# Input projection of a hybrid decoder step: groups of four 128-column items, 512 prompt columns per product, sample tokens as the stationary operand

## The reference, cut to what matters

```python
def mixer_inputs(x, norm_w, w_in, a_q_norm, a_k_norm):
    xn = rms_norm(x, norm_w)
    u, o, mz, ig, fg, q, kv, g, az = jnp.split(xn @ w_in, SPLIT_AT, axis=-1)
    q = rms_norm(q.reshape(B, T, A_HEADS, A_DH), a_q_norm)
    ...
    g = jax.nn.sigmoid(g).reshape(B, T, 3, A_HEADS)
```

## Time and profile before

| | us |
|---|---|
| median of 3 runs | 2227.49 (2226.57 to 2228.03) |
| the profiled execution | 2227.76 |
| its span in the trace | 2226.1 |
| PE busy | 2051.2, 92% of the span |
| DVE busy, ACT busy | 830.4 and 697.4 |
| first to last product of line 250 | 12.5 to 718.3 |

### The profile page before, as it was taken

How to read it: one execution, slowest core, us unless ns; L and a number is a source line. 1 busy time by engine, 2 the same in 40 slices (tenths; PEclk the granted TensorE clock), 3 DMA queues, 4 the chain that set the end, 5 groups by cost and what they waited for, 6 DMA issues and landing times. The chain is left out here.

```text
span 2226.1 us, 34268 instructions
## 1 busy us (share of the span) xinstructions
PE 2051.2 (92%) x13409; PEld 1658.3 (74%) x13409; DVE 830.4 (37%) x1639; ACT 697.4 (31%) x1328; POOL 50.7 (2%) x99
## 2 busy tenths in 40 slices
PE   7999999999999799968997799999997699999998
PEld 7999999999999455655554354544444599989997
DVE  6233235423332334526563134433334422242332
ACT  6332223333332222205663223332222321142222
POOL 0000000000000100000000000000000011100000
PEclk9999999999999788858998899999997799999999
DMA  5452233333331433220123768888864642223320
GB/s 190 163 187 79 87 98 98 107 102 107 99 112 53 155 140 140 82 106 29 58 75 128 262 221 277 294 298 301 301 243 152 228 147 77 81 86 107 99 73 22
DMA packets 163699, 315.00 MB, mean 142 GB/s; under 512 B 18893, under 2 KB 68430, under 8 KB 160466
## 3 DMA queue, kind: packets, MB, share of 16 engines
q1 hardware_dynamic: 143656, 278.98, 37.2%
q10 hardware_dynamic: 19882, 33.83, 4.3%
HBM read 280.75 MB, written 40.26 MB: 144 GB/s over the span
## 5 line engine op out<-in xcount | busy, mean ns | idle before, releaser
L250 PE MATMUL mm<-x_hi,w_hi 128*128 128x288 f32 x1696 | 368.3, 299 | 14.2 <-DVE w_lo L381 14.2
L250 PE MATMUL mm<-x_hi,w_lo 128*128 128x288 f32 x1696 | 363.9, 296 | 0.0
L250 PE MATMUL mm<-x_lo,w_hi 128*128 128x288 f32 x1696 | 363.8, 296 | 0.0
L250 PEld LDWEIGHTS mm<-x_hi,w_hi 128*128 128x128 f32 x1696 | 274.4, 189 | 15.8 <-issue 12.5
L250 PEld LDWEIGHTS mm<-x_hi,w_lo 128*128 128x128 f32 x1696 | 273.9, 189 | 0.0
L250 PEld LDWEIGHTS mm<-x_lo,w_hi 128*128 128x128 f32 x1696 | 273.8, 189 | 0.0
L381 DVE TENSOR_TENSOR w_lo<-w_raw,w_hi 128x1024 fp32r<-128x1024 f32 x106 | 129.8, 1225 | 384.8 <-ACT w_hi L280 384.8
L1515 PE MATMUL s_pH<-wide,cw_sample 128*128 128x512 f32 x512 | 244.5, 619 | 16.2 <-DMA wide<-pages 13.7
L1997 PE MATMUL o_mm<-o_feat_hi,o_w_hi 128*128 128x288 f32 x1024 | 224.7, 301 | 23.6 <-DVE o_feat_lo L2072 19.4
L1997 PE MATMUL o_mm<-o_feat_lo,o_w_hi 128*128 128x288 f32 x1024 | 221.0, 298 | 0.0
L1997 PE MATMUL o_mm<-o_feat_hi,o_w_lo 128*128 128x288 f32 x1024 | 220.7, 297 | 0.0
(11 more groups left out here) (402 smaller groups left out, 2296.3 us busy)
## 6 DMA issues: line engine op xcount, KB each, us to landing
wide<-pages SPq DMA_DIRECT2D x256, 256.0 KB, 3.6
w_raw<-w_in SPq DMA_DIRECT2D x106, 512.0 KB, 3.9
s_kv<-pages SPq DMA_DIRECT2D x128, 256.0 KB, 11.1
s_kv<-pages ACTq DMA_DIRECT2D x128, 256.0 KB, 8.1
o_w_raw<-w_out SPq DMA_DIRECT2D x16, 1024.0 KB, 8.6
o_w_raw<-ple_gate SPq DMA_DIRECT2D x16, 1024.0 KB, 6.7
m_state<-state SPq DMA_DIRECT2D x4, 2056.0 KB, 12.8
state_sample<-m_state SPq DMA_DIRECT2D x4, 2056.0 KB, 6.6
```

The lines of the kernel that those rows point to most:

```text
L250: last = nc.tensor.matmul(mm[:, s % 3, y, 0:HALF], w[:, m % RING, kk, :], f[:, k, y * HALF:(y + 1) * HALF], start=k == 0 and i == 0, stop= ...
```

## The change

The 53 items are put into 13 groups of four and one group with the gate item alone; val moves from behind the gate to the end. A unit is now 2 k-blocks of a group's 512 columns (the gate: 8 k-blocks of 128), still 512 KB, and there are still 106 of them: 8 for a group of four, 2 for the gate. The four items of a group accumulate side by side in four PSUM banks.

For the 512 prompt tokens PE runs one 512-column product where it ran two of 288: for each unit 4 items x 2 k-blocks x 3 = 24. For the 64 sample tokens the roles turn: x_hi and x_lo of the sample tokens are stationary (128 columns, the low part in new columns of `x_hi`), and the weights of the four items stream, 512 columns at once: for each k-block one "wide" product against w_hi and one with the 64 high columns against w_lo, so 4 per unit. They end in one bank (`tail`), token-major. ACT copies it to `sums` (`summed`), and PE turns it back with the stacked identity `stack`, which also adds the halves (`fold`, four float32 matmuls of 64 columns for each group); DVE then scales the result (`sample`). The gate's sample part is computed as before, as 48 products of 64 columns.

`lanes()` writes out which unit (slot) carries which step of which item. The rings are now raw 3, hi 3, lo 2, staging 5. The sum of squares for the norm is taken by PE after unit 2.

```diff
-        mm = ps("mm", [P, 3, 2, CH])
+        mm, tail, turned = ps("mm", [P, 4, CH]), ps("p_tail", [P, CH]), ps("p_turned", [P, 4, TSA])
...
+    for g, group in enumerate(GROUPS):
+        end = max(v for v, (x, _) in enumerate(UNITS) if x == g)
...
+            put(end, "prompt", base + i)
+        if not gate:
+            put(end + 1, "fold", g)
+            for i in range(len(group)):
+                put(end + 2, "sample", base + i)
+        for i in range(len(group)):
+            x = end + 2 * i + (8 if gate else 0)
+            put(x + 2, "first", base + i)
+            put(x + 3, "aside", base + i)
+            put(x + 4, "second", base + i)
+            put(x + 5, "store", base + i)
...
+            def fold(g):
+                pe.wait_ge(sums_ready, nfold(g))
...
+                for i in range(4):
+                    last = nc.tensor.matmul(turned[:, i, :], sums[:, i * P:(i + 1) * P], stack[:], start=True, stop=True)
...
+            def unit(m):
...
+                pe.wait_ge(whi_done, m + 1)
+                pe.wait_ge(wlo_done, m + 1)
+                for i in range(n):
+                    if c == 0 and g:
+                        free = start_of(g - 1) + min(i + 1, len(GROUPS[g - 1]))
+                        pe.wait_ge(prompt_out, free)
...
+                        for y, (w, x) in enumerate(((hi, xhi), (hi, xlo), (lo, xhi))):
+                            last = nc.tensor.matmul(mm[:, i, :], w[:, kk, own], x[:, k, 0:TP], start=k == 0 and y == 0, stop=k == KD - 1 and y == 2)
...
+                if n == 4:
+                    for k, wide in ((ks[0], c == 0), (ks[1], c == 0), (ks[0], c > 0), (ks[1], c > 0)):
+                        if wide:
+                            last = nc.tensor.matmul(tail[:], xhi[:, k, TP:T + TSA], hi[:, k % 2, :], start=k == 0, stop=k == KD - 1)
+                        else:
+                            last = nc.tensor.matmul(tail[0:TSA, :], xhi[:, k, TP:T], lo[:, k % 2, :], start=False, stop=False)
...
+                last.then_inc(unit_done, 1)
+
+            for s in range(LAST + 1):
+                if s < NU:
+                    unit(s)
+                if s == 2:
                     pe.wait_ge(ones_ready, 1)
                     pe.wait_ge(added, KD - 1)
...
             def low(m):
-                if m >= 2 * NI:
+                if m >= NU:
                     return
                 dve.wait_ge(whi_done, m + 1)
-                if m >= RING:
-                    dve.wait_ge(half_done, m - RING + 1)
-                v.tensor_tensor(wlo[:, m % RING], raw[:, m % RING], whi[:, m % RING].bitcast(F32), ALU.subtract).then_inc(wlo_done, 1)
+                if m >= LO:
+                    dve.wait_ge(unit_done, m - LO + 1)
+                v.tensor_tensor(wlo[:, m % LO], raw[:, m % RAW], whi[:, m % HI].bitcast(F32), ALU.subtract).then_inc(wlo_done, 1)
...
+            def prompt(j):
                 kind, n = ITEMS[j]
-                dve.wait_ge(half_done, 2 * j + 2)
...
+                dve.wait_ge(item_done, j + 1)
...
+                v.tensor_tensor(dst, src, rstd[:, 0:TP], ALU.mult).then_inc(prompt_out, 1)
...
             def first(j):
                 kind, n = ITEMS[j]
+                if kind == "u":
+                    convolve(j)
                 if kind in ("u", "z", "az"):
                     dve.wait_ge(sig_ready, nth(("u", "z", "az"), j))
...
+            for s in range(2, LAST + 1):
+                low(s + 2)
+                for what, j in LANES.get(s, []):
+                    if what == "prompt":
+                        prompt(j)
+                    elif what == "sample":
+                        sample(j)
+                    elif what == "first":
+                        first(j)
+                    elif what == "second":
+                        second(j)
```

More of the change, by code:

```diff
@@ L188, in _ @@
                 sp.dma_start(x[:, 4 * i:4 * i + 4, :], a["x_fm"][:, 4 * i:4 * i + 4, :]).then_inc(x_in[i], 16)
[L189 to L199, removed]
+                load(i)
+            for s in range(LAST + 1):
+                load(s + 3) if s else None
+                for what, j in LANES.get(s, []):
+                    if what == "store":
+                        store(j)
+                if s % 2 == 0 and 8 <= s < 8 + 2 * NB:
+                    sp.dma_start(o["win_kept"][s // 2 - 4], a["win_rows"][s // 2 - 4, TS:WIN, :]).then_inc(B.win_kept, 16)
+            for i in range(SLOTS):
+                sp.wait_ge(kv_out[i], 16 * sum(1 for j in range(NI) if ITEMS[j][0] in STORED and j % SLOTS == i))
             sp.wait_ge(row_out, 32 * nth(("o", "z"), NI - 1))
@@ L216, in aside @@
                     pe.wait_ge(sq_ready, nth(NORMED, j))
-                    for h in range(2):
-                        last = nc.tensor.matmul(aux[:, h, 0:HALF], pair[:], sq[:, h * HALF:(h + 1) * HALF], start=True, stop=True)
+                    for part, out in both(sq):
+                        last = nc.tensor.matmul(out, pair[:], part, start=True, stop=True)
                 elif kind == "gate":
@@ L231, in aside @@
                         dst = aux[0:w, t // 4, (t % 4) * P:(t % 4) * P + P]
-                        last = nc.tensor.transpose(dst, stg[:, j % 3, t0:t0 + w], B.ident[:])
+                        last = nc.tensor.transpose(dst, stg[:, j % SLOTS, t0:t0 + w], B.ident[:])
                 last.then_inc(aux_done, 1)
[L235 to L253, removed]
@@ L254, in _ @@
+            for s in range(LAST + 1):
+                if s < NU:
+                    unit(s)
+                if s == 2:
                     pe.wait_ge(ones_ready, 1)
                     pe.wait_ge(added, KD - 1)
-                    for y in range(2):
-                        last = nc.tensor.matmul(aux[:, y, 0:HALF], B.ones[:], rk[:, y * HALF:(y + 1) * HALF], start=True, stop=True)
+                    for part, out in both(rk):
+                        last = nc.tensor.matmul(out, B.ones[:], part, start=True, stop=True)
@@ L323, in second @@
                         act.wait_ge(normal, nth(NORMED, j) - 1)
-                    last = s_.activation(halved(rk[:]), aux[:, :, 0:HALF], ACT.Ln, bias=B.eps[:, 0:1], scale=1.0 / AD)
+                    for part, read in both(rk):
+                        last = s_.activation(part, read, ACT.Ln, bias=B.eps[:, 0:1], scale=1.0 / AD)
                     last.then_inc(aux_read, 1)
@@ L357, in _ @@
                     high(3)
-            high(4)
             act.wait_ge(ssq_done, 1)
-            step(s_.activation(halved(rstd[:]), aux[:, :, 0:HALF], ACT.Ln, bias=B.eps[:, 0:1], scale=1.0 / D))
+            for part, read in both(rstd):
+                last = s_.activation(part, read, ACT.Ln, bias=B.eps[:, 0:1], scale=1.0 / D)
+            step(last)
             s_.activation(rstd[:], rstd[:], ACT.Exp, scale=-0.5).then_inc(rs_ready, 1)
[L362 to L368, removed]
+            for s in range(2, LAST + 1):
+                high(s + 2)
+                for what, j in LANES.get(s, []):
+                    if what == "fold":
+                        summed(j)
+                    elif what == "first":
+                        first(j)
+                    elif what == "second":
+                        second(j)
         @block.vector
@@ L428, in convolve @@
                 empty(j)
+                dve.wait_ge(prompt_out, j + 1)
                 dve.wait_ge(evac, j + 1)
```

188 lines of the change are left out of this document (128 added, 60 removed).

## The result

| | before | after |
|---|---|---|
| median, us | 2227.76 (2226.57 to 2230.68) | 2325.85 (2322.97 to 2325.91) |
| span of the profiled execution | 2226.1 | 2324.1 |
| last product of the projection starts | 718.3 | 811.8 |
| next stage's first instruction | 725.49 | 821.69 |

The ratio is 1.0438, interval 1.0425 to 1.0451: the change makes the kernel 98 us slower, where 49.5 slower was forecast (2277), and the result lies 6 us above the range. Of the 98, 93.5 are there by the last product (after: the second of a pair that starts at 811.60), and the stages behind the projection take 2.6 of the rest.

The account below looks back on a forecast made before the run. The prediction took PE's stream of products as the projection's only bound. Products -33.4, folds +14, group starts +56 (standing plus clock), first 50 us +7.9 and end +5 gave +49.5 on 2227.76: forecast 2277 us, range 2240 to 2320.

Parts of the forecast that it names:

- products, gate included: PE's projection products: 2960 at 0.216 us plus 48 short ones, 645.8 against 679.2 before, so -33.4 us.
- folds: PE's 13 x 4 float32 matmuls turning the sample sums, with switches between kinds: +14 us, between 8 and 20.
- standing at group starts: PE waits at 13 group starts for DVE's eviction, behind `low` and earlier steps: 50.3 us in sum.
- clock behind them: Half clock on PE after the two u-group stops of 8.8 us, 2.9 each: +5.8 us, nothing for the others.
- first 50 us: Projection start: later x and `w_lo`, PE waiting 6.3 us for the additions, then half clock: +7.9 us, between 4 and 9.
- end: Stage's end: val comes last, so DVE's evictions and the transposes follow the last product: +5 us, between 2 and 8.
- the first rival: PE's products: 0.0135 us is a fixed cost of every `fp32r` product, 0.227 each; total 2310 us, chance 0.13.
- The cold row: Profile row from PE's cold start: 288 columns in 0.240 us, columns at 1.2 GHz and no more.
- The rival without standing: Group starts: DVE has evicted before PE needs the bank, so the 56 us go; 2221 us, chance 0.08.

Follow-up runs that it names:

- sums_first: `evict_first` plus unit 4's weights prepared earlier, the norm's sum after unit 3, and ACT's copy of sample sums ahead of the last u sigmoids: 2239.79 us, ratio 1.0058.
- forms: The changed kernel with 24 extra products of varied number form and width ahead of each fold, to price them: fp32r of 512 columns 0.228 us each.
- after_again: The changed kernel executed once more without any edit, to compare the clock behind the same 13 stops: 2323.32 us.
- evict_first: The changed kernel with DVE doing the eviction and the steps it needs ahead of `low` in each group's last slot: 2261.8 us, ratio 1.0173.
- lo3: The changed kernel with three slots of `w_lo` instead of two and two of raw weights instead of three, DVE's order unchanged: 2258.37 us, ratio 1.0151.

## Why the prediction came out where it did

| term | forecast | measured | from |
|---|---|---|---|
| products, gate included | -33.4 | +0.5 | 104 x 6.38 + 48 x 0.2267 + 48 x 0.110 against 679.2 |
| folds | +14 (13) | +9.6 (12) | 7.18 - 6.38 each in `sums_first`; the 13th is in the end |
| standing at group starts | +50.3 | +52.7 | 50.5 idle and 13 x 0.17 of drain |
| clock behind them | +5.8 | +21 | the same stretches in `sums_first` are 73.6 shorter; less 52.7 |
| first 50 us | +7.9 | +7.5 | unit 4 at 50.27, 12.0 beyond 12.8 + 4 x 6.38; less 4.8 before; 0.3 for 12.8 against 12.5 |
| end | +5 | +1.9 | 95.4 at the next stage's first product, less 93.5 |
| other stages | 0 | +2.6 | 98.0 of span less 95.4; the output projection alone +3.9, the others less |
| not assigned | | +2 | |

**Products: the step that failed first, 34 of the 48.5 us missed.** The prediction took 0.216 for an `fp32r` product of 512 columns, and 0.2267 was measured. The two facts it rested on were right: 0.0135 beside the columns in the old products, next to nothing in a pass of a float32 matmul. The error was to carry the float32 pass over to `fp32r` because both read 4 bytes a column, and to explain the 0.0135 away as a load that 288 columns don't cover. `forms` shows it to be a fixed time of `fp32r`, from 256 to 512 columns; that is the first rival, to which the prediction gave a chance of 0.13. That one put the term at -1, and +0.5 was measured. The cold row that spoke for it was the nearer evidence, being of the same number form. The sum shows why nothing is gained. Fewer products carry less of the fixed time (5088 x 0.0135 = 69 before, 2960 x 0.0133 = 39 after: -29). But 53,000 more columns are streamed (+22), the gate's 48 short products pay the floor of 0.110 (+4), and a unit has 0.03 at its switches (+3). The prediction had 8 in place of the 39 (2960 x 0.0027).

**Clock: the second, 15 us.** The forecast put a price only behind the two stops of 8.7 us, and nothing behind the eleven shorter ones, because in one row PE restarted at full pace after 2.90 us of idle time. Eleven of 13 stops lost 1.6 to 2.8 us each, both of 2.08 us among them, and `after_again` shows some of them the other way round. One restart was no bound for a cost that varies. The very stop of that row came out otherwise in the kernel after: the output projection, whose code is the same, stands at this place for 5.31 us and restarts at half clock. First PE of after, then two of its windows, to be set beside the earlier trace rows:

```profile
1889.45 0.82 PE L2103 MATMUL o_mm<-o_feat_hi,o_w_hi 128*128 128x288 f32 x2 [5.31 <-DVE o_w_lo L2172]
```
```profile
1888.00:1892.00 4.00, 2.55 (x11) 2.58 (x12) 2.01 (x2) 1.96 (x2) 1.19 (x1) 0.54 0.03 10
1892.00:1896.00 4.00, 4.00 (x21) 4.00 (x21) 2.29 (x1) 0.53 (x1) 0.24 (x1) 0.61 0.01 2
```

From the first to the last start of that line the stage takes 456.6 us, for 452.7 before. The same stop is 4.6 to 5.6 us long in every kernel made from the change, and a later one, at 2077.84, is 2.08 for 1.30 before. Why the first is 2.90 before was not settled.

**Right: where PE stands, and why.** All 13 stops, for the order and for the two slots; the first of 2.08 (2.2 forecast with 0.17 drain), the two behind u groups of 8.65 and 8.64 (8.8 forecast). `evict_first` and `lo3` take away the same stops from two sides. The DVE view at the longest one reads as the forecast had it, `low`, the convolution, the sigmoids' 2.18, the product, the eviction:

```profile
395.19 1.23 DVE L470 TENSOR_TENSOR w_lo<-w_raw,w_hi 128x1024 fp32r<-128x1024 f32 x1 [3.54 <-PE p_tail L315]
396.33 0.54 DVE L529 TENSOR_SCALAR p_stage<-upad,convw,convb 128x512 f32<-128x512 f32 x1
...
402.23 0.76 DVE L569 TENSOR_TENSOR p_stage<-p_stage,p_square 128x576 f32<-128x576 f32 x1 [2.18 <-ACT p_square L399]
402.90 2.48 DVE L502 TENSOR_TENSOR upad<-mm,p_rstd 128x512 f32<-128x512 f32 x4
```

The rival without standing fell with this, and no wait came up inside the groups. The start (four units by 50.27, 49.7 forecast, a stop of 5.93 for 6.3) came as worked out, but for a slip in the prediction: 49.7 lies 13.0 beyond 12.5 + 4 x 6.05 and not 12.7. Folds and end were sized too high, 7.5 together, which took that much off the miss. What was not foreseen is the wait of `tail` for ACT's copy: hidden in `after` behind the longer stop, it costs 14 us once that is gone.

## What to carry to other kernels

Price a new shape from a row of the same number form (here `fp32r`), and take a residue beside the columns for a fixed cost until a row of that form shows it gone; then multiply by the columns too, since fewer products that stream more columns can come out even. Where a group of results shares all accumulators, evict before anything that waits for the same last product; moving the eviction in front of `low` was worth 60 us here and needed no buffer. In a dense stream of products a stop of 1.8 us or more should be priced with some 2 us of half clock behind it, as most of those here had, and a single stop of up to 1.66 us at its length. Short stops close together are another matter, as the last section shows.

## What the runs showed of the hardware

- An `fp32r` product of 256 to 512 columns takes its columns at 2.4 GHz and 0.013 to 0.016 us, and one of 64 to 192 columns 0.11; bf16 and the float32 passes lack the 0.013 (0.216 and 0.2145 for 512 columns).
- Stops of 0.88 and 1.66 us in a dense stream kept the clock nine times of nine. In the two executions of the change, whose stops last 2.08 to 8.65 us, 22 of 26 were followed by half clock (1.2 GHz), which cost 1.5 to 2.8 us; the four of 8.65 among them no more than the short ones (1.56, 2.79, 2.40, 1.60). In `forms` it was 12 of the same 13. The fall can come late: at 79 us in the view above, a microsecond after PE was busy again.
- Short stops close together lost the clock. In the stage's tail of `sums_first` PE stands for 0.69, 0.41 and 0.84 us between 730 and 734 us, with 1.10 and 0.74 us of work between them, and the granted clock is 0.69 in the window from 733 to 735 and 0.50 in the next:

```profile
735.00:737.00 2.00, 1.16 (x6) 0.87 (x5) 0.00 (x0) 0.75 (x2) 0.00 (x0) 0.50 0.52 196
```
